# One buffer for key and value rows: loaded early or written by the projection, outputs stored from it, index pages on three queues

## What is computed

```python
def _even_project(x, w_in):                      # layer 0
    qa, ka, va, ga, qkv, gb, ab, bb = _split_cols(x @ w_in, EVEN_COLS)
    ...
def _odd_project(x, w_in):                       # layer 1
    qc, kc, vc, gc, qi, ki, wi = _split_cols(x @ w_in, ODD_COLS)
    ...
def _index_select(qi, wi, ki, pos_q, k_sel):
    dots = jnp.einsum('bqhd,bkd->bqhk', qi, ki).astype(jnp.float32) * IDX_DIM ** -0.5
    score = jnp.einsum('bqh,bqhk->bqk', wi.astype(jnp.float32) * IDX_HEADS ** -0.5, jax.nn.relu(dots))
    admissible = jnp.arange(ki.shape[1])[None, :] <= pos_q[:, None]
    _, idx = lax.top_k(jnp.where(admissible, score, -jnp.inf), k_sel)
    return idx, idx <= pos_q[None, :, None]
...
    # outputs besides y_prompt, y_sample:
    # a_k, a_v (keys and values of layer 0), b_s, b_conv, c_k, c_v (of layer 1), c_idx, for prompt and samples
    # c_idx of the samples' past lies in pages: cache_c_idx[page_table], 16 pages of 128 positions for each sample
```

## Time and profile before

| | |
|---|---|
| median of 3 runs | 2730.76 us (2723.95 to 2739.94) |
| profiled execution | 2739.75 us, its span 2738.1 us |
| mean granted TensorE clock | 0.881 of full speed |
| TensorE matmuls busy | 2210.1 us, 81% |
| VectorE busy | 1165.0 us, 43% |
| ScalarE busy | 688.3 us, 25% |
| GpSimd busy | 244.5 us, 9% |

### The profile page before, as it was taken

The page is one execution under the profiler, slowest core; times in us unless marked ns, Lnnn a source line. Parts: engine busy times, 40 slices in busy tenths (PEclk is TensorE's granted clock), DMA queues, the critical chain, the costliest instruction groups (busy, mean ns, idle before and its releaser), DMA issues. The chain is left out here.

```text
span 2738.1 us, 30594 instructions
## 1 busy us (share of the span) xinstructions
PE 2210.1 (81%) x9786; PEld 1328.0 (49%) x9786; DVE 1165.0 (43%) x2443; ACT 688.3 (25%) x1588; POOL 244.5 (9%) x338
## 2 busy tenths in 40 slices
PE   7999897986888855889545999866999948884688
PEld 3444565655778734466313345523644326651333
DVE  1000000866666432899501111185899936620111
ACT  2221001222333301667300111061121126640011
POOL 0000000002332200100032000030000000003200
PEclk9999999998999855899867999987999969986699
DMA  7001111100000013000089401013000030007740
GB/s 237 32 31 42 54 46 31 37 0 11 9 9 8 6 35 94 16 16 17 3 269 304 132 23 54 8 51 112 22 23 34 37 102 24 16 3 241 252 157 39
DMA packets 133286, 180.60 MB, mean 66 GB/s; under 512 B 23104, under 2 KB 103392, under 8 KB 132112
## 3 DMA queue, kind: packets, MB, share of 16 engines
q1 hardware_dynamic: 98648, 130.30, 14.4%
q10 hardware_dynamic: 24640, 25.41, 2.9%
q0 software_dynamic: 9856, 23.13, 2.6%
HBM read 152.48 MB, written 30.70 MB: 67 GB/s over the span
## 5 line engine op out<-in xcount | busy, mean ns | idle before, releaser
L538 PE MATMUL banks<-actT 128*128 128x350 f32 (+1 forms) x960 | 285.3, 460 | 12.2 <-ACTq L548 12.2
L538 PEld LDWEIGHTS banks<-actT 128*128 128x128 f32 x960 | 183.7, 192 | 113.0 <-ACTq L548 12.4
L198 PE MATMUL banks<-fr_w,actT 128*128 128x512 f32 (+1 forms) x640 | 238.3, 530 | 0.0
L474 PE MATMUL banks<-ptg_w,heads 128*128 128x512 f32 (+1 forms) x432 | 185.8, 592 | 1.7 <-ACT heads L426 1.7
L2902 DVE TENSOR_SCALAR_CACHE_REDUCE ch_hits<-c_chosen,ch_cand 128x384 bf16<-128x384 f32 (+1 forms) x186 | 175.9, 946 | 18.0 <-DVE ch_cand L2907 12.2
L198 PEld LDWEIGHTS banks<-fr_w,actT 128*128 128x128 f32 x640 | 113.6, 193 | 125.6 <-issue 125.5
L2346 PE MATMUL banks<-a_pages,actT 128*128 128x512 f32 x384 | 166.3, 593 | 0.0
L474 PEld LDWEIGHTS banks<-ptg_w,heads 128*128 128x128 f32 (+1 forms) x432 | 77.7, 180 | 109.3 <-issue 109.3
L600 PE MATMUL banks<-actT,aq_w 128*128 128x350 f32 (+1 forms) x384 | 117.3, 464 | 12.2 <-DMA aq_w<-w_in_e_dram 12.2
L1722 ACT ACTIVATE aa_prob<-aa_prob,aa_mx 128x128 f32<-128x128 f32 (+7 forms) x128 | 98.1, 767 | 77.4 <-DVE aa_mx L1823 77.4
L2346 PEld LDWEIGHTS banks<-a_pages,actT 128*128 128x128 f32 x384 | 72.3, 190 | 88.9 <-issue 88.9
(11 more groups left out here) (517 smaller groups left out, 3528.3 us busy)
## 6 DMA issues: line engine op xcount, KB each, us to landing
tok_rows<-fr_stage SPq DMA_DIRECT2D x8, 1028.0 KB, 3.9
fr_w<-w_in_e_dram SPq DMA_DIRECT2D x8, 1024.0 KB, 21.5
actT<-w_in_e_dram SPq DMA_DIRECT2D x6, 1024.0 KB, 5.4
a_pages<-cache_a_k_dram SPq DMA_DIRECT2D x48, 128.0 KB, 4.3
a_pages<-cache_a_v_dram SPq DMA_DIRECT2D x48, 128.0 KB, 4.2
a_pages<-w_out_e_dram SPq DMA_DIRECT2D x3, 2048.0 KB, 13.0
ptg_w<-w_in_o_dram SPq DMA_DIRECT2D x3, 2048.0 KB, 13.1
c_pages<-cache_c_k_dram SPq DMA_DIRECT2D x48, 128.0 KB, 3.7
```

The source lines that it names most:

```text
L198: last = nc.tensor.matmul(m.ps[:, j, 0:g[1]], m.actT[:, c, t * P:t * P + P], weights[j][:, c, :], start=(c == 0), stop=(c == KC - 1))
L474: last = nc.tensor.matmul(m.ps[0:r, j, 0:g[1]], rows[:, slot, c, 0:r], weights[j][:, c, :], start=(c == 0), stop=(c == KC - 1))
L538: last = nc.tensor.matmul(m.ps[:, NS * j + k, 0:tn], wring[:, s, c, j * P:(j + 1) * P], m.actT[:, c, t0:t0 + tn], start=(c == 0), stop=(c ...
```

## The change

1. A buffer `m.kv_rows` (128 partitions x 9 tiles x 512 columns) stays allocated from the first block behind the front to the end. Key rows are its first 256 columns, value rows (`m.v`) the others.
2. Layer 0: `fetch_kv` loads it at the end of SyncE's gate loads in `delta_prompt` with two DMAs; VectorE clears its last tile at the start of that block. `turn_keys` has only the transposes and the copies.
3. Layer 1: in `token_programs` the last group (keys and values) is written by ScalarE into the buffer instead of the stage (`kept`), and isn't stored to `tok_rows`. Behind the last tile TensorE transposes the keys (`tensor_keys`) and ScalarE copies them (`scalar_keys`). VectorE clears the last tile ahead of its search.
4. The outputs are stored from the buffer in `prompt_attention`, six DMAs behind the gate load of tile 2. Both `store_kv` blocks and both `load_kv` blocks are gone.
5. Until it is needed, the buffer holds the weight ring of `feature_units`; in `middle` it holds the residual rows of the first four tiles. Four work matrices of `delta_prompt` lie in free columns of `actT`. The samples' new values come from the buffer.
6. Index pages: six on SyncE, five on ScalarE, five on GpSimd for each sample. ScalarE issues two behind each of the first 20 pairs of relus.

```diff
 def token_programs(own, nc, m, w, groups, tok, tag, two=True, rows=None, kept=None):
...
     for j, g in enumerate(groups):
+        if kept is not None and j == len(groups) - 1:
+            continue
...
-                nc.scalar.activation(stage[0:r, slot, starts[j]:starts[j] + groups[j][1]],
-                                     m.ps[0:r, j, 0:groups[j][1]], ACT.Silu if groups[j][3] else ACT.Copy)\
+                if kept is not None and j == len(groups) - 1:
+                    if isinstance(t, int) and t == FULL:
+                        act.wait_ge(m.kv_cleared, 2)
+                    dst = kept[0:r, bass.ds(t, 1), :].rearrange("p o c -> p (o c)")
+                else:
+                    dst = stage[0:r, slot, starts[j]:starts[j] + groups[j][1]]
+                nc.scalar.activation(dst, m.ps[0:r, j, 0:groups[j][1]], ACT.Silu if groups[j][3] else ACT.Copy)\
...
+    def tensor_keys(pe):
+        pe.wait_ge(act_out, n_act * (NT + 1))
+        key_tiles(nc, m).then_inc(product, 1)
+
+    def scalar_keys(act):
+        act.wait_ge(product, len(groups) * NT + 1)
+        for dst, bank in turned_keys(m):
+            nc.scalar.copy(dst, bank)
...
+                fetch_kv(sp, m, m.tok)
                 sp.wait_ge(z["state_out"], NT + 1)
...
             @block.vector
             def _(dve):
+                dve.memset(m.kv_rows[:, FULL, :], 0.0).then_inc(m.kv_cleared, 1)
...
+def fetch_kv(sp, m, tok):
+    sp.wait_ge(m.kv_cleared, 1)
+    src = tok[:, TOK_K:TOK_K + 2 * KV * P]
+    sp.dma_start(m.kv_rows[:, 0:FULL, :], src[0:FULL * P].rearrange("(t p) c -> p t c", p=P)).then_inc(m.kv_in, 16)
+    sp.dma_start(m.kv_rows[0:LAST, FULL, :], src[FULL * P:T]).then_inc(m.kv_in, 16)
...
+def store_kv(sp, m, outs):
+    for prompt, samples, rows in outs:
+        sp.dma_start(prompt[0:FULL * P].rearrange("(t p) c -> p t c", p=P), rows[:, 0:FULL, :]).then_inc(m.s_out, 16)
+        sp.dma_start(prompt[FULL * P:L], rows[0:TAIL, FULL, :]).then_inc(m.s_out, 16)
+        sp.dma_start(samples, rows[TAIL:LAST, FULL, :]).then_inc(m.s_out, 16)
...
+                    if p.t == 2:
+                        store_kv(sp, m, outs)
...
-    SP_PAGES = 9
+    SP_PAGES, ACT_PAGES = range(0, 6), range(6, 11)
+    POOL_PAGES = range(11, N_PAGES)
...
+                mine = [(p, q, j) for p in range(PAIRS) for q in range(2) for j in ACT_PAGES]
                 for n, (t, a) in enumerate(pairs):
...
+                    for k in range(2 * n, min(2 * n + 2, len(mine))):
+                        load_page(act, *mine[k], s["pages_act"])
...
+        def clear(dve):
+            dve.memset(m.kv_rows[:, FULL, :], 0.0).then_inc(m.kv_cleared, 1)
+        run(nc, [load_bits, t_load, f_load, t_store], [f_pe, f_out, t_pe, t_turn], [f_act, t_act, t_keys],
+            [clear, search])
```

More of the change, by code:

```diff
@@ L366, in _, with token_programs @@
                 program(dve)
-def token_programs(own, nc, m, w, groups, tok, tag, two=True, rows=None):
+def token_programs(own, nc, m, w, groups, tok, tag, two=True, rows=None, kept=None):
     starts = [sum(g[1] for g in groups[:j]) for j in range(len(groups))]
@@ L390, in token_programs @@
     rows = E(nc.sbuf_tensor(f"{tag}_rows", [P, 2, KC, P], F32)) if rows is None else rows
-    stage = E(nc.sbuf_tensor(f"{tag}_stage", [P, 2, width], F32))
+    stage = E(nc.sbuf_tensor(f"{tag}_stage", [P, 2, max(b for _, b, _ in stores)], F32))
     w_in = [m.sem(f"{tag}_w_in{j}") for j in range(len(groups))]
@@ L479, in tensor @@
         over_tiles(pe, tile)
-    return load, store, tensor, scalar, vector
+    def tensor_keys(pe):
[5 more added lines that the diff above has]
+            nc.scalar.copy(dst, bank)
+    return load, store, tensor, scalar, tensor_keys, scalar_keys
 def project_features(nc, m, w, parts, tag, ready=None):
@@ L1447, in _ @@
                 nc.vector.tensor_tensor(out, o[:], rs[:].rearrange("p (b h) -> p b h", h=B_H), ALU.mult)
[L1452 to L1467, removed]
-            @block.tensor
-            def _(pe):
-                pe.wait_ge(kv_in, 64)
-                for g in range(KV):
-                    for t in range(NT):
-                        r = P if t < FULL else LAST
-                        last = nc.tensor.transpose(m.ps[:, 3 * g + t // 4, t % 4 * P:t % 4 * P + r],
-                                                   k[0:r, t, g * P:(g + 1) * P], m.ident[0:r, 0:r])
-                last.then_inc(turned, 1)
-            @block.vector
-            def _(dve):
-                dve.memset(m.v[:, FULL, :], 0.0).then_inc(cleared, 1)
-                dve.wait_ge(turned, 1)
-                for g in range(KV):
-                    for j in range(3):
-                        n = min(512, T - 512 * j)
-                        nc.vector.tensor_copy(m.kT[:, g, 512 * j:512 * j + n], m.ps[:, 3 * g + j, 0:n])
@@ new lines, in key_tiles, with turned_keys, turn_keys, _ @@
+def key_tiles(nc, m):
+    for g in range(KV):
+        for t in range(NT):
+            r = tile_rows(t)
+            last = nc.tensor.transpose(m.ps[:, 3 * g + t // 4, t % 4 * P:t % 4 * P + r],
+                                       m.k_rows[0:r, t, g * P:(g + 1) * P], m.ident[0:r, 0:r])
+    return last
+def turned_keys(m):
+    for g in range(KV):
+        for j in range(3):
+            n = min(512, T - 512 * j)
+            yield m.kT[:, g, 512 * j:512 * j + n], m.ps[:, 3 * g + j, 0:n]
+def turn_keys(nc, m):
+    turned = m.sem("kv_turned")
+    with nc.Block() as block:
+        @block.tensor
+        def _(pe):
+            pe.wait_ge(m.kv_in, 32)
+            key_tiles(nc, m).then_inc(turned, 1)
+        @block.vector
+        def _(dve):
+            dve.wait_ge(turned, 1)
+            for dst, bank in turned_keys(m):
+                nc.vector.tensor_copy(dst, bank)
@@ L2392, in middle @@
         sb = lambda name, shape: E(nc.sbuf_tensor("md_" + name, shape, F32))
-        h, scaled = sb("h", [P, NT, D]), m.heads[:, 6:8, 0:D]
+        scaled, later = m.heads[:, 6:8, 0:D], sb("h", [P, NT - 4, D])
+        early = m.kv_rows[:].rearrange("p a b -> p (a b)")[:, 0:4 * D].rearrange("p (t d) -> p t d", d=D)
+        h = [early[:, t, :] if t < 4 else later[:, t - 4, :] for t in range(NT)]
         ss, rstd, gain = sb("ss", [P, NT]), sb("rstd", [P, NT]), sb("gain", [P, KC])
@@ L2720, in _ @@
                     for q in range(2):
-                        for j in range(SP_PAGES):
+                        for j in SP_PAGES:
                             load_page(sp, p, q, j, s["pages_sp"])
@@ L2727, in _ @@
                     for q in range(2):
-                        for j in range(SP_PAGES, N_PAGES):
+                        for j in POOL_PAGES:
                             load_page(pool, p, q, j, s["pages_pool"])
```

84 lines of the change are left out of this document (39 added, 45 removed).

## The result

The changed kernel took 2684.53 us (median of 3 runs, 2684.37 to 2688.77) against 2730.76: a ratio of 0.984, 95% interval 0.9814 to 0.9865. The forecast was 2687. The profiled execution has a span of 2682.7 us against 2738.1, so the traces differ by 55.4 and the medians by 46.2: the execution that was traced of before (2739.75) is the longer end of its three, and part of what the two traces differ by is not the change.

What follows compares the result with a forecast made beforehand. TensorE computes nearly all the time, so removals count only where every engine waits; SyncE's queue ends the index-page wait. Terms sum to -43.7 us, from the median 2730.76 to 2687; own range 2678 to 2696, 8-in-10 range 2670 to 2708.

Steps and rivals of the forecast that it cites:

- output block, layer 0: After the first layer's projection: removing the output stores and barrier lets TensorE start at 284.6, -4.4 us (-3.6 to -4.9).
- reload, layer 0: Before the first attention: rows loaded early in the delta stage, transposes right after the barrier, -9.2 us (-8.0 to -9.3).
- search to first load, layer 1: Before the second attention: reload and output block go, transposes and copies hidden beside the search, -21.7 us (-20.5 to -21.9).
- load to bias products, layer 1: Second attention's start: bias and flip loads no longer share DMA engines with 2 MB of output, -1.7 us (0 to -1.8).
- memset ahead of the search: Layer 1: new memset of 512 columns on VectorE, the bound engine, ahead of the threshold search, +0.5 us.
- stores in the attention: Six output DMAs behind tile 2's gate load: about 3 us of issue, cost 0, at most 1 if a gate is delayed.
- first relu to page products: Index stage: pages on three queues let TensorE start page products at 1866.5 instead of 1873.68, -7.2 us.
- A pair then takes 2.38 + 0.25: Index stage on ScalarE: two page issues plus passing two relus and a wait, 2.63 us per pair, 52.6 for 20.
- With drained buffers, 30: Index stage: the last eight relu pairs, 31.1 us in the kernel before, would take 30 us.
- The smaller edits have the same answer, 0: New token's values from the buffer, split residual rows and matrices in free columns of actT would cost 0.
- The list of what would show it: Expected trace signs, including pairs 2.6 us apart and TensorE's page products some 15 us behind SyncE's last page, waiting for relus.

Runs made afterwards that it cites:

- a2: Kernel before with only the index pages spread over three queues (six, five, five): 2716.83 us against 2732.05, ratio 0.995.
- b4: Changed kernel with each layer's six output stores in a block of their own ahead of the attention, still out of the buffer: 2694.40 us, ratio 0.9869.
- a3: Changed kernel with layer 1's key transposes and copies in their own block behind the threshold search instead of beside it: 2693.64 us, ratio 0.9867.
- c0: Changed kernel run again, unaltered: 2686.23 us against 2732.22, ratio 0.9833.
- b3: Changed kernel with layer 0's key and value rows fetched behind the delta stage, in the block of the key transposes: 2699.08 us, ratio 0.9877.
- d1: Kernel before with layer 1's output block moved ahead of its key and value reload: 2734.84 us against 2734.56, ratio 1.0004.
- a1: Changed kernel with index pages on two queues, nine of sixteen on SyncE and seven on GpSimd: 2699.40 us, ratio 0.9882.
- b1: Changed kernel with index pages on two queues, seven of sixteen on SyncE and nine on GpSimd: 2683.87 us, ratio 0.9822.
- b2: Changed kernel with index pages split seven on SyncE, one on ScalarE, eight on GpSimd: 2681.62 us, ratio 0.9811.
- c1: Changed kernel with index pages seven SyncE, one ScalarE, eight GpSimd, ScalarE's eight issued behind pairs 20 to 23: 2678.59 us, ratio 0.9803.
- a4: Changed kernel with ScalarE waiting for both relus of a pair to complete before issuing that pair's two pages: 2711.95 us, ratio 0.9939.

## Why the prediction was right, term by term

The time was right, and each of the large terms has the mechanism that was forecast. Two terms were too small and one cost was missing; the index pages are the second largest gain, where the forecast had them third. That the sum came within 3 us is in part luck, since these misses have opposite signs. Measured are stretches of the traces, old code against new (a2 counts as new in the last row):

| term | forecast | old executions | new executions | measured |
|---|---|---|---|---|
| output block, layer 0 | -4.4 | 7.05 to 7.19 | 2.79 to 2.81 | -4.3 |
| reload, layer 0 | -9.2 | 9.16 to 9.40 | 0 | -9.3 |
| search to first load, layer 1 | -21.7 | 22.17, 22.56 | 0.89 | -21.5 |
| load to bias products, layer 1 | -1.7 | 8.23, 8.85 | 5.85 to 6.66, mean 6.0 | -2.5 |
| memset ahead of the search | +0.5 | 312.43 to 312.46 | 312.87 to 312.90 | +0.4 |
| stores in the attention | 0 | | (b4) | 0 |
| first relu to page products | -7.2 | 88.99 to 89.96, mean 89.6 | 77.3 to 79.3, mean 78.4 | -11.2 |

- *Barriers and reloads.* The block was rightly priced by what stands between its first issue and the next engine's start, not by its issue time alone. The early fetch hid its memset: VectorE idles 4.28 us behind the two.
- *Layer 1.* a3 shows the cover. Two sizes were off in the safe direction: the transposes take 2.45 and not 4.33, and ScalarE's six copies 2.22 and not 4.1; no table load was needed.
- *Contention.* The step "the loads of bias and flip then no longer share the DMA engines with 2 MB of output" was right in its place and too small in its bound: 2.5 against at most 1.8. The bound came from one execution of layer 0, 6.48, and layer 1's own wait without the copies is 6.0.
- *Index pages.* The mechanism was right: ScalarE's page at 1.19 us, the DMA instruction at 0.484, relus beside it. The size was off by 4: "A pair then takes 2.38 + 0.25": the passing of two relus and a wait costs 0.15, so 2.53, which is 2.0 us over 20 pairs. "With drained buffers, 30" for the last eight pairs: 28.3 here, another 1.7. Among the kernels with this split their time goes with the granted clock, which the forecast left out: 28.3 to 28.4 us at a mean of 0.76 (after, c0, b3), 26.6 to 26.9 at 0.80 to 0.81 (a2, a3, b4). That spread makes up the rest of the 4. Where few or no pages are issued in the 20 pairs ahead (before, d1, a1, b1, b2, c1) the last eight take 31.1 to 32.7 at 0.73 to 0.78, which the clock alone does not explain; what drained buffers have of it no run separates.
- *Stores in the attention.* The cost of 0 held (b4), though the six take 5.8 us to issue (2197.76 to 2203.58) and not "about 3"; nothing waited for SyncE there.
- *The missing cost.* "The smaller edits have the same answer, 0" was wrong for the new token's values. Read from the buffer, that load occupies SyncE for 0.80 us in place of 0.30, the next for 0.46 in place of 0.26, and the sample attention's second batch of pages leaves 11.4 us behind its first in place of 10.6. TensorE starts on it 21.2 to 22.0 us behind the first page in place of 20.2 to 20.7: about +1. No run takes this one edit back, so the cause is read from the queue and not tested. SyncE's queue after, and then before:

```profile
1367.15 0.80 SPq L2181 DMA_DIRECT2D sa_vnew<-kv_rows  x1
1367.98 0.46 SPq L2182 DMA_DIRECT2D sa_gate<-tok_rows  x1
```
```profile
1388.98 0.30 SPq L2144 DMA_DIRECT2D sa_vnew<-tok_rows  x1
1389.67 0.26 SPq L2145 DMA_DIRECT2D sa_gate<-tok_rows  x1
```

The terms sum to -48.4, with the missing cost -47.4; the stage behind the index scores also starts 0.7 sooner behind the page products (9.8 in place of 10.5 us), which makes -48.1. The medians give -46.2 and -46.0. In five of eleven traces of new code the stretch from the sample attention's first load to the index stage's is 396 us in place of 393.5; the three of old code have 392.3 to 392.8. Averaged over the eleven that is 1.1 us more, half of the gap. The 2.5 us arise ahead of `middle`'s first residual (VectorE's first `md_h`), where TensorE waits for a DMA of output weights; the first of these weight loads is issued 111.5 to 113.5 us behind the first page in all new traces and 110.1 to 110.4 in the old. So a delay of 1 to 3 us reaches SyncE's queue there in every new trace, and the wait hides a part of it. Whether all of it comes from the missing cost above stays open.

The list of what would show it held but for one number: TensorE starts 21.7 us behind SyncE's last page, for which the forecast's own figures (1842 and 1866.5) give 24.5 and not the 15 that it wrote.

## What to carry to other kernels

Price a removed stage at every engine's barrier, from the traces, and a queue's extra work by what the same engine does at that place: an issue beside work longer than it is nearly free, beside shorter work it sets the pace. Before adding a third queue look at when the two others end: here moving two of SyncE's nine pages to GpSimd shortened the stage by 4.5 us more in the traces than the third queue did. Compare stretches between landmarks over several executions rather than two spans; here chance made 9 of 55 us.

## What the runs showed of the hardware

- Four copies from DRAM to DRAM, 2 MB in all, make what waits for the loads behind them 1.6 to 2.8 us later (before, a2, d1). Behind six stores of the same data out of SBUF the issue of the two loads takes 0.4 us longer, and the wait, 6.34 us, lies inside the 5.85 to 6.66 of the traces without them (b4).
- The load of the samples' eight value rows occupies SyncE's queue for 0.80 us with its source in SBUF (0.79 to 0.80 in eleven traces) and for 0.30 with its source in DRAM (three traces). Other few-row loads were not compared.
- The last pairs of the index stage run at two paces: in the changed kernel their starts are 5.1 to 5.7 us apart and then 3.98, with a mean granted clock of 0.66 in the window, a mix of the two levels; in a4 they are 4.11 and then 3.98 apart at 1.00, 2.4 GHz, though TensorE had idled more there:

```profile
1822.00:1842.00 20.00, 12.14 (x48) 2.63 (x48) 12.44 (x11) 7.52 (x8) 0.00 (x0) 0.66 0.00 0
```
```profile
1854.00:1868.00 14.00, 5.92 (x42) 1.54 (x37) 11.10 (x9) 7.74 (x8) 0.00 (x0) 1.00 0.00 0
```

The first is the changed kernel, the second a4. Why the clock was full behind more idle time no run here tells.
